# A two-block transformer kernel: a ninth buffer for expert weights, selection masks built for four experts at a time, the first expert loads reordered, and mask additions on GpSimd cut in pieces

## What is computed

```python
def one_row(args):                                # neighbourhood attention
    ...
    s = s + jnp.transpose(bias, (0, 2, 1, 3)).astype(jnp.float32)[None]
    s = jnp.where(col_in[None, None, :, None, :], s, MASK_VALUE).reshape(B, H, GRID_W, kh * GRID_W)
    ...
def hierarchical_moe(h, w_rg, b_rg, w_re, b_re, w_gate, w_up, w_down):
    ...                                           # comb: weight of each expert for each token, 2 of 16 not zero
    def one_group(args):                          # four experts of one group
        wg_g, wu_g, wd_g, comb_g = args
        hid = jax.nn.silu(jnp.einsum('td,edf->tef', t, wg_g)) * jnp.einsum('td,edf->tef', t, wu_g)
        return jnp.einsum('tef,efd->td', hid * comb_g[:, :, None], wd_g)
    y = jnp.sum(lax.map(one_group, (wg, wu, wd, jnp.moveaxis(combine, 1, 0))), axis=0)
```

## Time and profile before

| | |
|---|---|
| median of 3 runs | 800.99 us (800.65 to 801.05) |
| the profiled execution's own time | 800.54 us |
| its span, first to last instruction | 798.5 us |
| PE busy | 754.6 us, 95% of the span |
| DVE, ACT, POOL busy | 410.3, 310.9, 24.9 us |
| DMA traffic | 198.96 MB, mean 249 GB/s over the span |
| the chain that ended last | PE 74%, DMA 13%, DVE 8%, ACT 3% |
| largest single item of that chain | `DMA ring<-in_w_up`, 11.2% |

### The profile page before, as it was taken

How to read it: one execution, slowest core, us unless ns; L and a number is a source line. 1 busy time by engine, 2 the same in 40 slices (tenths; PEclk the granted TensorE clock), 3 DMA queues, 4 the chain that set the end, 5 groups by cost and what they waited for, 6 DMA issues and landing times.

```text
span 798.5 us, 11488 instructions
## 1 busy us (share of the span) xinstructions
PE 754.6 (95%) x4534; PEld 527.0 (66%) x4534; DVE 410.3 (51%) x730; ACT 310.9 (39%) x554; POOL 24.9 (3%) x22
## 2 busy tenths in 40 slices
PE   4999999998997999999899999999899999999997
PEld 2597784444695443453253347887788999999885
DVE  2682704579646111221021138767557888888443
ACT  3453203545625001010010035745446666666433
POOL 0000110022000000000000000020000000000000
PEclk9999999999999999999999999999999999999999
DMA  9882203978468997999999996205302544585201
GB/s 372 353 324 113 70 36 119 357 273 339 178 263 354 372 427 315 431 428 425 428 428 419 421 427 261 105 0 219 124 2 106 211 158 164 204 355 219 111 0 53
DMA packets 19242, 198.96 MB, mean 249 GB/s; under 512 B 2144, under 2 KB 2528, under 8 KB 3840
## 3 DMA queue, kind: packets, MB, share of 16 engines
q1 hardware_dynamic: 18288, 194.80, 60.7%
q0 software_dynamic: 624, 3.28, 1.0%
q10 hardware_dynamic: 288, 0.30, 0.1%
HBM read 197.32 MB, written 1.05 MB: 248 GB/s over the span
## 4 chain that ended last, share of the span: by engine, by line
PE 74%; DMA 13%; DVE 8%; ACT 3%; issue 1%; SPq 0%; DVEq 0%; ACTq 0%
DMA ring<-in_w_up 11%; PE banks L1534 10%; PE banks L1124 8%; PE banks L1812 7%; PE banks L1787 6%; PE banks L1791 5%; PE banks L1795 5%; PE banks L1570 4%; PE banks L1082 3%; PE banks L1321 2%; DVE w_lo L1861 2%; DMA ring<-in_w_mod 2%; PE banks L1150 2%; PE banks L1154 2%; PE banks L1152 2%; PE banks L1341 2%
## 5 line engine op out<-in xcount | busy, mean ns | idle before, releaser
L1861 DVE TENSOR_TENSOR w_lo<-ring,w_hi 128x1024 fp32r<-128x1024 f32 (+1 forms) x122 | 145.9, 1202 | 78.5 <-ACT w_hi L702 27.5
L1534 PE MATMUL banks<-ring,att 128*64 128x512 f32 x512 | 117.8, 601 | 8.7 <-DMA ring<-in_w_up 4.3
L1534 PEld LDWEIGHTS banks<-ring,att 128*64 128x64 f32 x512 | 41.3, 138 | 83.3 <-issue 71.5
L702 ACT ACTIVATE w_hi<-ring 128x1024 fp32r<-128x1024 f32 x50 | 52.0, 1053 | 37.0 <-PE banks L1124 23.3
L2227 DVE TENSOR_TENSOR lat<-lat,banks 128x512 f32<-128x512 f32 x8 | 5.5, 688 | 106.9 <-PE banks L1534 106.9
L1787 PE MATMUL banks<-h_hi,w_hi 128*128 128x256 f32 x352 | 51.6, 286 | 0.7 <-ACT h_hi L1017 0.7
L994 ACT ACTIVATE w_hi<-ring 128x1024 fp32r<-128x1024 f32 x44 | 46.3, 1053 | 14.1 <-PE banks L1795 14.1
L1791 PE MATMUL banks<-h_hi,w_lo 128*128 128x256 f32 x352 | 50.2, 286 | 0.0
L1795 PE MATMUL banks<-h_lo,w_hi 128*128 128x256 f32 x352 | 49.9, 285 | 0.0
L1787 PEld LDWEIGHTS banks<-h_hi,w_hi 128*128 128x128 f32 x352 | 46.0, 192 | 2.2 <-ACT h_hi L1017 1.2
L1791 PEld LDWEIGHTS banks<-h_hi,w_lo 128*128 128x128 f32 x352 | 46.2, 195 | 0.0
(11 more groups left out here) (367 smaller groups left out, 1453.1 us busy)
## 6 DMA issues: line engine op xcount, KB each, us to landing
ring<-in_w_up SPq DMA_DIRECT2D x21, 2048.0 KB, 10.9
ring<-in_w_mod SPq DMA_DIRECT2D x11, 2048.0 KB, 8.9
ring<-in_w_gate SPq DMA_DIRECT2D x10, 2048.0 KB, 16.3
ring<-in_w_down SPq DMA_DIRECT2D x9, 2048.0 KB, 16.7
ring<-in_w_in SPq DMA_DIRECT2D x8, 2048.0 KB, 17.7
ring<-in_w_gate SPq DMA_DIRECT2D x12, 1024.0 KB, 9.5
ring<-in_w_up SPq DMA_DIRECT2D x12, 1024.0 KB, 11.1
ring<-in_w_down SPq DMA_DIRECT2D x9, 1024.0 KB, 17.1
```

Source lines behind the costliest of these rows:

```text
L702: nc.scalar.activation(chunk_part(w_hi, chunk, c), chunk_src(chunk, c), ACT.Copy).then_inc(chunk_hi[stage], 1)
L1534: last = nc.tensor.matmul(bank[2 + j][CAP * e:CAP * (e + 1), :], xs[:, k, at:at + CAP], slot(n + e, KD)[:, k, :], start=(k == 0), stop=(k ...
L1861: return V.tensor_tensor(dst, src, high.bitcast(F32), ALU.subtract)
```

## The change

The edits, by name of what they touch:

- `odd_gate`: a ninth place for a tile, in `front` (a new tensor that joins `rstd`, the rope constants and `lat`) and in the end of `arena`, made larger by 256 columns. It takes the gate tile of expert 0 of each odd pair, as two halves. `hid`, `modp2`, `logit_parts`, `wr_x`, `pick_w` move to other addresses.
- The order of the expert loads (`even_pair`, `odd_pair`). An even pair: gate 0 without a wait, the four halves of the down tiles, then gate 1, up 0, up 1. An odd pair: the two halves of the new place without a wait, gate 1, up 0, up 1, down 0, down 1.
- The first loads: `gate_load(1, 0)` ahead of `w_out`, `gate_load(1, 1)` ahead of pair 0's gate 1; up half 5 of pair 0 and down half 8 of pair 1 issued after six of eight parts of the output projection; for that, `chunk_part` turns the places of the chunks of the first block by one.
- `picks_r` holds four experts' selection (512 columns) instead of sixteen's. DVE rebuilds it in each odd pair that is followed by another, with two TENSOR_TENSOR of 256 columns.
- POOL's mask additions in pieces of 256 columns: 8 and 8 for the bias, 4 and 4 in the second block. Its DMAs share one semaphore.
- The second load of the constants is split in two (388 and 896 columns).

```diff
             sp.wait_ge(ATT[0]["pv"], 4)
             for j in (8, 10):
                 spare_load(0, j)
+            gate_load(1, 0)
             for n in range(2):
                 issue(L_OUT + n, w_out[n])
...
             sp.wait_ge(ATT[0]["pv"], 8)
             spare_load(0, 11)
+            gate_load(1, 1)
...
+            sp.wait_ge(proj_out, 6)
+            expert_load(0, 5)
+            expert_load(1, 8)
             sp.wait_ge(proj_out, KD)
-            for j in (5, 7):
-                expert_load(0, j)
+            expert_load(0, 7)
             spare_load(0, 9)
-            for j in range(8, 12):
+            for j in (10, 9, 11):
                 expert_load(1, j)
...
-            def expert_tile(i, stage, e):
+            def expert_tile(i, stage, e, freed=None):
                 n = L_MOE + 2 * stage + e
+                if freed is not None:
+                    sp.wait_ge(used, freed + (4 * stage + e + 3))
...
+            def even_pair(i, freed):
+                expert_tile(i, 0, 0)
+                for j in range(8, 12):
+                    sp.wait_ge(used, freed + (j + 1))
+                    spare_load(i, j)
+                for stage, e in ((0, 1), (1, 0), (1, 1)):
+                    expert_tile(i, stage, e, freed + 12)
+
+            def odd_pair(i, freed):
+                for half in range(2):
+                    gate_load(i, half)
+                for stage, e in ((0, 1), (1, 0), (1, 1)):
+                    expert_tile(i, stage, e, freed + 12)
+                for e in range(2):
+                    expert_tile(i, 2, e)
...
             def rest_of_window(done):
-                expert_loads(1, done, range(8))
-                for j in range(8, 12):
-                    sp.wait_ge(used, done + (j + 1))
-                    spare_load(2, j)
-                whole_tiles(2, range(2), done + 12)
+                expert_loads(1, done, (1, 3, 4, 5, 6, 7))
+                even_pair(2, done)
                 with sp.Fori(0, 2) as i:
-                    whole_tiles(i * 2 + 3, range(2), i * 24 + (done + 24))
-                    whole_tiles(i * 2 + 3, (2,), None)
-                    whole_tiles(i * 2 + 4, range(2), i * 24 + (done + 36))
-                    for j in range(8, 12):
-                        spare_load(i * 2 + 4, j)
-                expert_loads(7, done + 72)
+                    odd_pair(i * 2 + 3, i * 24 + (done + 12))
+                    even_pair(i * 2 + 4, i * 24 + (done + 24))
+                for half in range(2):
+                    gate_load(7, half)
+                expert_loads(7, done + 72, (1, 3, 4, 5, 6, 7))
+                expert_loads(7, done + 60, range(8, 12))
...
-                nc.gpsimd.tensor_tensor(b, b, namask.unsqueeze(1).broadcast_to([P, 32, GRID_W]),
-                                        ALU.add).then_inc(bias_ready, 1)
+                for i in range(0, 32, 4):
+                    ins = nc.gpsimd.tensor_tensor(b[:, i:i + 4, :], b[:, i:i + 4, :],
+                                                  namask.unsqueeze(1).broadcast_to([P, 4, GRID_W]), ALU.add)
+                ins.then_inc(bias_ready, 1)
...
+                    if gathers:
+                        dve.wait_ge(picked, w * 8 + d * 2 + 2)
+                        for q in range(NT):
+                            ins = V.tensor_tensor(pick_t[:, q], bc(iota, 1, [P, 4, CAP]),
+                                                  bc(posm[:, bass.ds(d * 4 + (NE * q + 4), 4)], 2, [P, 4, CAP]), ALU.is_equal)
+                        ins.then_inc(picked_t, 1)
```

More of the change, by code:

```diff
@@ L87 @@
 CON, NCON = columns([("upper", 128), ("ones", 128), ("pick4", 4), ("pick8", 8), ("pick20", 20), ("ident", 128), ("tri", 128),
[L88 to L90 removed]
+                     ("namask", 64), ("desc", 4), ("iota", 64),
+                     ("same", 128), ("turn", 128), ("rot", 128), ("cos", T), ("sin", T)])
+CON_FIRST, CON_ROPE = CON["ident"], CON["same"]
+NROPE = NCON - CON_ROPE
 PROD = ([("ql", i, "AD"[i % 2]) for i in range(3)] + [("naq", i, "AD"[i % 2]) for i in range(4)]
@@ L318, in block_pair_kernel @@
         namask = con[:, CON["namask"]:CON["namask"] + 64]
-        same, turn, rot = (con[:, CON[name]:CON[name] + P] for name in ("same", "turn", "rot"))
-        cos, sin = (con[:, CON[name]:CON[name] + T] for name in ("cos", "sin"))
+        same, turn, rot = (rope[:, CON[name] - CON_ROPE:CON[name] - CON_ROPE + P] for name in ("same", "turn", "rot"))
+        cos, sin = (rope[:, CON[name] - CON_ROPE:CON[name] - CON_ROPE + T] for name in ("cos", "sin"))
         iota = con[:, CON["iota"]:CON["iota"] + CAP]
@@ L369, in block_pair_kernel @@
         landed_spare = [sem(f"landed_spare{half}") for half in range(2)]
+        landed_gate = [sem(f"landed_gate{half}") for half in range(2)]
         used = sem("used")
@@ L530, in spare_load, with gate_load, expert_loads @@
                 expert_load(i, j, (spare(e, half), landed_spare[half]))
-            def expert_loads(i, before, js=range(12)):
+            def gate_load(i, half):
+                expert_load(i, 2 * half, (odd_gate(half), landed_gate[half]))
+            def expert_loads(i, freed, js):
                 for j in js:
-                    sp.wait_ge(used, before + (j + 1))
+                    sp.wait_ge(used, freed + (j + 1))
                     expert_load(i, j)
-            def expert_tile(i, stage, e):
+            def expert_tile(i, stage, e, freed=None):
@@ L590, in _ @@
                         spare_load(0, j)
+                    for half in range(2):
+                        gate_load(1, half)
                     expert_loads(1, w * 96 + 84, range(8, 12))
@@ L1511, in arrived @@
                     at = slot_of(n)
-                    if n < L_MOE + 4 and half == 0:
+                    if n == L_MOE and odd:
+                        pe.wait_ge(landed_gate[half], w * 64 + d * 16 + 16)
+                    elif n == L_MOE and half == 0:
+                        pe.wait_ge(landed[at], w * 64 + d * 16 + landed_count(n))
+                    elif n == L_MOE and halves:
+                        pe.wait_ge(landed_later[at], w * 16 + 32)
+                    elif n < L_MOE + 4 and half == 0:
                         pe.wait_ge(landed[at], w * 128 + d * 32 + (16 * odd + landed_count(n)))
                     elif n < L_MOE + 4 and halves:
-                        pe.wait_ge(landed_later[at], w * 48 + (16 * min(2 * d + odd + 1, 3) + 16 * (at == slot_of(L_QL))))
+                        pe.wait_ge(landed_later[at], w * 48 + 16 * min(2 * d + odd + 1, 3))
                     elif half == 0:
@@ L1519, in arrived, with gate_or_up @@
                         pe.wait_ge(landed_later[at], w * 32 + 16 * min(d + 1, 2))
+                def gate_or_up(n, k, odd):
+                    if n == L_MOE and odd:
+                        return odd_gate(k // 4).rearrange("p (k n) -> p k n", n=FE)[:, k % 4, :]
+                    return slot(n, KD)[:, k, :]
                 def expert_pair(d, odd, gathers, first=False, halves=False):
@@ L2242, in _ @@
                 inputs(w * 16 + 4, 3, 6)
-                for q in range(NT):
-                    V.tensor_tensor(pick_t[:, q, 4:NE], bc(iota, 1, [P, NE - 4, CAP]),
-                                    bc(slots[:, q, 4:NE], 2, [P, NE - 4, CAP]), ALU.is_equal).then_inc(picked_t, 1)
-                dve.wait_ge(picked_t, w * 3 + 3)
-                V.tensor_scalar(posm[:, :], posm[:, :], -float(CAP), None, ALU.add).then_inc(posm_moved, 1)
                 with dve.Fori(0, NPAIR // 2 - 1) as d:
```

99 lines of the change are left out of this document (52 added, 47 removed).

## The result

The changed kernel takes 803.89 us (median of 20 runs, 801.12 to 807.8), the kernel before 801.18 us beside it. The ratio is 1.0029, 95% interval 1.0019 to 1.0040: slower by 2.3 us (1.5 to 3.2). On another chip it was 805.09 against 801.35 us, 1.0040 (1.0025 to 1.0055). The forecast was 804.6. The profiled execution took 803.41 us, forecast 804.1.

A forecast was written before the change was run, and what follows sets the result against it. Experts bound by the weight stream, PE needing nearly as long; 3.9 us lost less 0.3 gained takes the profiled 800.54 to 804.1 us, and the median, 0.45 above, to 804.6. Range of 8 in 10: 799.5 to 807.5.

The forecast's parts named there:

- The ninth place and the gap: Expert weight stream: two halves of lead, 5.0 us, less 1.7 us of idle stream near 323 us, leaves 3.3 us.
- The order of loads: Even expert pairs: pair 6's up tiles end at half 84, not 80, landing 6.7 us later; experts end 3.9 us later.
- Slow clock behind the waits: PE's gate work in pairs 4 and 6: up to 3 us of slowness costs nothing; taken as zero, 2 us in range.
- The pieces and `w_out`: First attention: pieces remove 3.8 us of PE stalls, the later `w_out` takes the gain back; 0.3 us gain taken.
- rival 2: Attention stalls stay gone: up to 3.8 us kept, 801.1 us; half of it 802.7; chance 0.2 for 799.5 to 802.6.
- The sum: Whole kernel: 3.9 us lost in the experts less 0.3 gained in the attention, 3.6 us slower.
- Rival 1: Experts: the stream's lead reaches the end, so the change is faster; 795.7 us with neither gap nor order counting; chance 0.15.

The follow-up runs named there:

- the second profile: The changed kernel unchanged, profiled again on the other chip, where it took 805.09 us against 801.35 for the kernel before.
- the order of use: Changed kernel with even pairs loaded gate 0, gate 1, up 0, up 1, then the four down halves: 799.72 us, ratio to before 0.9982.
- both edits: Changed kernel with even pairs' down halves loaded last and the ninth place's first half issued behind `w_out`: 795.26 us, ratio to before 0.9926.

## Why the prediction was right, and where it was not

**The ninth place and the gap.** The wait for pair 2's up tiles ended at 321.21 (1.2 us sooner than before), and the first up tile landed 8.05 us later, at 329.26; I had 7.7 and 330.1. The gap near 323 us is there.

**The order of loads.** Forecast: pair 6's up tiles at 434.3; measured 434.46. The hidden parts: a half took (434.46 - 329.26) / 42 = 2.505 us, not 2.48, which is 1.0 us more over 42 halves, and the first tile 0.35 us more; the start of 1.2 us sooner makes up for it. That it met to 0.2 us is luck: 2.0 us of those 42 halves are late landings, and the second profile has 432.98, with 2.470 us per half. The mechanism is not luck. Four halves more ahead of the up tiles are 9.9 us in the prediction and 9.1 by the runs, and the lead of the ninth place is 3.3 in the prediction and 2.3 to 2.5 by them. Last down half forecast at 464.1, measured 464.10. End of the experts forecast at 475.0, measured 474.9. The waits in pairs 4 and 6 were forecast at some 5 us and 2 to 3, measured 4.96 and 3.78, and 1.3. Corrected, the up tiles are 5.5 us late but the end of the experts only 473.5 - 471.0 = 2.5: before, the last pair waited for its own up tiles once more, until 457.38, and the changed kernel does not.

**Slow clock behind the waits.** I took zero, with 2 us in the range. In pair 6 the gate matmuls took 9.72 instead of 7.1 us, 2.6 lost, under the 3 us of slack; in pair 4, 8.49. Zero was right, with 1.35 us to spare, the wait for the up tiles that was left behind the slow gate work. Gate 1 moved ahead shows what it costs without that cover: 1.8 us.

**The pieces and `w_out`.** The sum was nearly right, -0.3 us forecast; at PE's first use of `w_out` the changed kernel is 201.66 - 1.4 = 200.3 against 201.23, -0.9. The two parts of it were mis-sized. I let the wait for `w_out` take away what PE had won ("from there on all is where it was"), and put the loss without the pieces at 1.5 us. The runs show a gain of 2.8 to 3.2 us for the pieces in the kernel before and of 2.4 to 3.3 in the changed one (cleaned and corrected), and a loss of 2.1 to 2.4 us, cleaned, for the half ahead of `w_out`. The failed step is that ACT's delay was carried to PE one for one, where PE had slack in its row. It did no harm to the forecast only because the two errors cancel. Two slips bear on bounds alone: the first half into `big` took 7.1 us to land where I wrote 6.8, and half of rival 2 is 803.0, not 802.7.

**The sum.** Forecast +3.6 us; measured +2.3 and +3.2 by the two ratios. The one profiled execution, at +2.9 in its own time, has three pieces of luck in it: 1.4 us at the start (against it), 1.4 us near 208 us (for it), and 1.1 us near 606 us (for it):

```profile
604.00:606.00 2.00, 1.99 (x7) 0.62 0.00 0
606.00:608.00 2.00, 2.00 (x11) 0.53 0.00 0
```

These two rows are of before; after, the clock is 1.00 there. Without the three it would be near +4.0.

**The rivals.** Rival 1 (the lead reaches the end) was wrong for this order; where pairs 4 and 6 keep their old order, 2.3 to 2.5 us of the lead do reach the end. Rival 2 (the stalls stay gone) is what the pieces do by themselves. What I did not see is that pair 2's down halves were early before too, and why: they fill the stretch near 287 us.

## What to carry to other kernels

When a stream bounds a stage, count what stands in the queue ahead of the transfer that is waited for last, not what the stream carries in all. Loading something early that is needed late is free only while the stream would otherwise be idle. Before an experiment is called the old order, compare its issues with the old kernel's in every pair, the first one too. A kernel with two changes that help (the pieces, the ninth place) and two that hurt reads as "a little slower"; each part had to be run alone to see that the pieces alone are worth 0.45%. The best versions here, 795.3 to 795.8 us, are the changed kernel with even pairs in the order of use (or with the early down halves in pair 2 alone) and the ninth place's first half behind `w_out`; the runs do not tell them apart.

## What the runs showed of the hardware

The granted clock of TensorE differs between executions of the same code at the same place. Before the 144 matmuls near 43 us an execution is either on time or 1.3 to 1.9 us late. And the same wait of 1.1 us, at PE's second use of `w_out`, was followed by the slow clock in one execution and not in the other (before, then after):

```profile
208.20 3.41 PE L1341 MATMUL banks<-osb,arena 128*64 128x256 f32 x16 [1.12 <-ACT osb L790]
```

```profile
208.66 1.95 PE L1374 MATMUL banks<-osb,arena 128*64 128x256 f32 x16 [1.15 <-ACT osb L823]
```

With the clock at 1.2 GHz for most of them the 16 matmuls took 3.41 us, at 2.4 GHz 1.95. The kernels with pieces alone and with both edits are a closer pair still: at both uses of `w_out` their waits are the same (1.01 and 1.16 us, 1.03 and 1.16), and the matmuls of the second took 3.29 us in one and 1.95 in the other. The wait's length alone doesn't decide it. A difference of 1 to 2 us between two single profiles of this kernel says nothing until these places have been compared.

POOL's addition in eight pieces took 6.28 us where one instruction took 4.79, and DVE's work beside it 1.92 us instead of 5.16: between pieces DVE gets its turn, as the prediction took it, though the two instructions were still twice as long as alone (0.88 us).
